# Compression blocks of two attention layers built by VectorE during the layer's projections, whose low weight parts VectorE also makes

## What is computed

```python
def nsa_mixer(h, w_in, cmp_pe, cmp_w1, cmp_w2, w_out):
    parts = jnp.split(h @ w_in, bounds, axis=-1)
    q = parts[0].reshape(B, T, NSA_KV, NSA_REP, NSA_DK)
    kc, vc, ks, vs, kw, vw = [p.reshape(B, T, NSA_KV, NSA_DK) for p in parts[1:7]]
    ...
    n_cmp = (T - CMP_LEN) // CMP_STRIDE + 1
    tok_idx = cmp_start[:, None] + jnp.arange(CMP_LEN)[None, :]

    def compress(a, j):
        blk = a[:, tok_idx] + cmp_pe[j][None, None, :, None, :]
        blk = jnp.moveaxis(blk, 3, 2).reshape(B, n_cmp, NSA_KV, CMP_LEN * NSA_DK)
        return jax.nn.gelu(blk @ cmp_w1[j]) @ cmp_w2[j]

    k_cmp = compress(kc, 0)
    v_cmp = compress(vc, 1)
```

## Time and profile before

| what | us or share |
|---|---|
| median of three runs | 3643.68 |
| lowest, highest | 3641.83, 3653.52 |
| the profiled execution's own time | 3645.8 |
| its span in the trace | 3644.0 |
| TensorE (PE) busy | 3038.3 (83%) |
| VectorE (DVE) busy | 2383.8 (65%) |
| ScalarE (ACT) busy | 1260.3 (35%) |
| GpSimd (POOL) busy | 590.9 (16%) |
| mean granted TensorE clock | 0.891 |

### The profile page before, as it was taken

The page is one execution under the profiler, slowest core; times in us unless marked ns, Lnnn a source line. Parts: engine busy times, 40 slices in busy tenths (PEclk is TensorE's granted clock), DMA queues, the critical chain, the costliest instruction groups (busy, mean ns, idle before and its releaser), DMA issues. The chain is left out here.

```text
span 3644.0 us, 52173 instructions
## 1 busy us (share of the span) xinstructions
PE 3038.3 (83%) x21162; PEld 2552.9 (70%) x21162; DVE 2383.8 (65%) x4291; ACT 1260.3 (35%) x2037; POOL 590.9 (16%) x321
## 2 busy tenths in 40 slices
PE   7977865565555699889999988999997999997899
PEld 4856752222211398868989876998986898987798
DVE  3677748888898687356767725877726775434654
ACT  1043211111111234264343445343345434343633
POOL 1010025555455100400000050000050000031000
PEclk9988777877767899879999987999997999996999
DMA  8932229999999786415758431867651764542153
GB/s 338 386 134 94 83 87 376 388 388 388 391 419 409 304 341 235 164 36 216 310 205 339 183 140 61 350 241 302 255 186 70 297 254 175 185 183 93 48 197 126
DMA packets 123103, 854.19 MB, mean 234 GB/s; under 512 B 17300, under 2 KB 18580, under 8 KB 21012
## 3 DMA queue, kind: packets, MB, share of 16 engines
q1 hardware_dynamic: 85748, 582.69, 41.7%
q0 software_dynamic: 36864, 268.45, 18.0%
q10 hardware_dynamic: 288, 0.26, 0.0%
HBM read 850.24 MB, written 1.11 MB: 234 GB/s over the span
## 5 line engine op out<-in xcount | busy, mean ns | idle before, releaser
L268 PE MATMUL ps<-h_hi,w_hi 128*128 128x256 f32 x3328 | 956.5, 287 | 51.8 <-DVE h_lo L459 26.2
L193 DVE TENSOR_TENSOR w_lo<-w_ring,w_hi 128x2048 fp32r<-128x2048 f32 x284 | 650.0, 2290 | 469.8 <-ACT w_hi L188 468.0
L269 PE MATMUL ps<-h_lo,w_hi 128*128 128x256 f32 x3328 | 952.0, 286 | 0.0
L270 PE MATMUL ps<-h_hi,w_lo 128*128 128x256 f32 x3328 | 951.7, 286 | 0.0
L188 ACT ACTIVATE w_hi<-w_ring 128x2048 fp32r<-128x2048 f32 x330 | 629.7, 1913 | 658.4 <-PE ps L270 646.5
L268 PEld LDWEIGHTS ps<-h_hi,w_hi 128*128 128x128 f32 x3328 | 645.1, 194 | 62.0 <-DVE h_lo L459 29.0
L269 PEld LDWEIGHTS ps<-h_lo,w_hi 128*128 128x128 f32 x3328 | 645.2, 194 | 3.2
L270 PEld LDWEIGHTS ps<-h_hi,w_lo 128*128 128x128 f32 x3328 | 644.8, 194 | 0.0
L193 POOL TENSOR_TENSOR w_lo<-w_ring,w_hi 128x2048 fp32r<-128x2048 f32 x46 | 212.2, 4631 | 2200.5 <-ACT w_hi L188 2200.5
L2937 PE MATMUL ps<-expert_rows,expert_diag 128*128 128x512 f32 x412 | 288.8, 841 | 231.2 <-ACT expert_diag L2978 231.2
L2937 PEld LDWEIGHTS ps<-expert_rows,expert_diag 128*128 128x128 f32 x412 | 92.2, 246 | 420.5 <-ACT expert_diag L2978 342.8
(11 more groups left out here) (461 smaller groups left out, 4232.2 us busy)
## 6 DMA issues: line engine op xcount, KB each, us to landing
w_ring<-in_w_stream SPq DMA_DIRECT2D x376, 1024.0 KB, 4.9
a_ring<-in_a_stream SPq DMA_DIRECT2D x108, 1024.0 KB, 7.0
a_ring<-in_t_stream SPq DMA_DIRECT2D x36, 1024.0 KB, 10.0
a_ring<-in_m_stream SPq DMA_DIRECT2D x8, 1024.0 KB, 7.3
alibi<-in_alibi SPq DMA_DIRECT2D x3, 2048.0 KB, 8.4
cond_row<-in_cond_row SPq DMA_DIRECT2D x8, 512.0 KB, 3.8
expert_rows<-in_experts,expert_idx POOLq DMA_INDIRECT x206, 11.8
gates<-mod_rows SPq DMA_DIRECT2D x3, 1024.0 KB, 5.1
```

The lines of the kernel that those rows point to most:

```text
L193: pool.tensor_tensor(self.w_halves(n)[1], self.w_item(n), self.w_halves(n)[0], ALU.subtract).then_inc(self.lo_made, 1)
L268: pe.matmul(out, stationary[0], moving[0], start=start, stop=False)
L269: pe.matmul(out, stationary[0], moving[1], start=False, stop=False)
L270: return pe.matmul(out, stationary[1], moving[0], start=False, stop=stop)
```

## The change

In the two `nsa` layers VectorE makes the low parts of items 3 to 10 during the projections, and GpSimd makes none there. VectorE puts each low part where ScalarE has the high one: ahead of unit n comes the low part of item n+3. The `cmp_blk` tile is taken before the projections. Behind its copy of unit 5 VectorE builds the 32 pieces of the keys' blocks (ScalarE's copy of unit 4 holds their source), and behind its copy of unit 7 the 32 pieces of the values' blocks. The compression block holds no additions and TensorE does not wait for blocks in it. The projections of the other two layers and the other stages are as before.

```diff
-def projections(core, items, units, side=None, split=True, ahead=S_AHEAD, tables=(), led=0, consts=()):
+def projections(core, items, units, side=None, split=True, ahead=S_AHEAD, tables=(), led=0, consts=(), beside=None):
...
         def copy(eng, parity):
-            ahead_of = splits if parity == 0 else range(0)
+            split = core.split_lo if parity else core.split_hi
+            ahead_of = splits if parity == 0 or beside else range(0)
             for u, (item, _, _, out) in enumerate(units):
                 while ahead_of and ahead_of[0] < first + item + S_SLOTS:
-                    core.split_hi(eng, ahead_of[0])
+                    split(eng, ahead_of[0])
                     ahead_of = ahead_of[1:]
...
                     out(eng, parity == 0, core.ps[:, u % BANKS, :]).then_inc(copied[parity].sem, 1)
+                    if beside and parity:
+                        beside(eng, u, copied)
             for n in ahead_of:
-                core.split_hi(eng, n)
+                split(eng, n)
...
-            for n in splits:
+            for n in () if beside else splits:
                 core.split_lo(pool, n)
...
+            blk = core.sb(early, "cmp_blk", [P, 2, CMP_LEN // 2, NSA_KV * N_CMP])
+
+            def blocks(dve, u, copied):
+
+                if u not in BLOCKS_BEHIND:
+                    return
+                i = BLOCKS_BEHIND.index(u)
+                for by in range(2):
+                    dve.wait_ge(copied[by].sem, copied[by].at(KEY_UNIT // 2 + 1))
+                if i == 0:
+                    dve.wait_ge(consts.sem, consts.at(32))
+                build_blocks(dve, blk, srcT, pe_col, i)
+
...
+KEY_UNIT = 4
+BLOCKS_BEHIND = (KEY_UNIT + 1, KEY_UNIT + 3)
+
+
+def build_blocks(dve, blk, srcT, pe_col, i):
+    for c in range(CMP_LEN // 2):
+        for up in range(2):
+            part = slice(up * DH, (up + 1) * DH)
+            t0 = 2 * c + up
+            src = srcT[i][part, :, t0:t0 + (N_CMP - 1) * CMP_STRIDE + 1:CMP_STRIDE]
+            dst = blk[part, i, c, :].rearrange("p (g n) -> p g n", g=NSA_KV)
+            dve.tensor_scalar(dst, src, pe_col[part, i, c:c + 1], None, ALU.add)
...
         @block.tensor
         def _(pe):
             for i in range(2):
-                pe.wait_ge(blocks.sem, blocks.at(i + 1))
                 for part in range(2):
```

More of the change, by code:

```diff
@@ L1545, in nsa_stage @@
             consts = core.semaphore_of("cmp_consts")
+            blk = core.sb(early, "cmp_blk", [P, 2, CMP_LEN // 2, NSA_KV * N_CMP])
[8 more added lines that the diff above has]
+                build_blocks(dve, blk, srcT, pe_col, i)
             projections(core, NSA_PROJ, units, ahead=0, tables=[(core.alibi[:], "alibi")], led=LEAD,
-                        consts=[(pe_col[:], core.io["cmp_pe"][j], consts), (w2[:], core.io["cmp_w2"][j], consts)])
-            compress(core, n, srcT, pe_col, w2)
+                        consts=[(pe_col[:], core.io["cmp_pe"][j], consts), (w2[:], core.io["cmp_w2"][j], consts)],
+                        beside=blocks)
+            compress(core, n, blk, w2)
             core.taken_whole()
@@ L1551, in nsa_stage, with compress @@
         out_projection(core, n.oT, 1, 1, 2, tail_room(core.alibi, n.ksT))
-def compress(core, n, srcT, pe_col, w2):
+KEY_UNIT = 4
[8 more added lines that the diff above has]
+            dve.tensor_scalar(dst, src, pe_col[part, i, c:c + 1], None, ALU.add)
+def compress(core, n, blk, w2):
     nc = core.nc
-    consts, blocks = core.semaphore_of("cmp_consts"), core.semaphore_of("cmp_blocks")
+    consts = core.semaphore_of("cmp_consts")
     hid, act_h, outs = core.semaphore_of("cmp_hid"), core.semaphore_of("cmp_act"), core.semaphore_of("cmp_outs")
@@ L1561, in compress @@
     nb = NSA_KV * N_CMP
-    chunks = CMP_LEN // 2
     with ExitStack() as ctx:
-        blk = core.sb(ctx, "cmp_blk", [P, 2, chunks, nb])
         hT = flat(n.oT)[:, 0:4 * nb].rearrange("p (i m n) -> p i m n", i=2, m=2)
@@ L1574, in _ @@
             core.dve_steps.done(dve, dve.memset(n.vcmp[:], 0.0))
[L1575 to L1584, removed]
             for i in range(2):
@@ L1637, in compress @@
     consts.passed(32)
-    for s in (blocks, hid, act_h, outs):
+    for s in (hid, act_h, outs):
         s.passed(2)
```

## The result

| | before | the change |
|---|---|---|
| median (lowest to highest), us | 3643.53 (3641.37 to 3653.52), 8 executions | 3628.81 (3610.00 to 3633.64), 8 executions |
| ratio to before, 95% interval | | 0.9949 (0.9937 to 0.9961) |
| profiled execution: time, span, us | 3645.8, 3644.0 | 3625.27, 3623.5 |

The kernel is 0.5% faster, 14.7 us. The forecast was 28 us, for a clock that holds through the compression in both layers. Half of that came: it is the time of the rival "holds in one layer" (3627), and the trace shows that rival, layer by layer.

What follows compares the result with a forecast made beforehand. TensorE's standing still, chiefly 10.45 us a layer for `cmp_blk`, and its half-clock compression were taken as the bound; +7.3 - 9.3 + 1.7 - 13.8 = -14.1 us a layer gave 3615.5 us, range 3608 to 3640.

Steps and rivals of the forecast that it cites:

- holds in one layer: Compression: full clock kept in one layer, lost at the other's entry; -17 us in all, 3627 us; chance 0.20.
- the one with 0.55: Compression: the clock holds at 1.00 through both halves in both layers, giving 3615.5 us; chance 0.55.
- VectorE's chain: Projections: low parts of items 8 and 10 queue behind additions, TensorE stalls 3.5 and 4.9 us; +7.3 us a layer.
- The clock in the projections: Item 10, behind the second stall: a stretch at half clock loses 1.7 us a layer, bounds 0 and 3.4.
- The entry: Between projections and compression: the wait of 10.45 us becomes a gap of 1.15; -9.3 us a layer.
- The compression's speed: Compression at full clock: 7.0 us a half, at most 8.1; 27.8 us become 14.0, -13.8 us a layer.
- The rule that I set against it: Compression: two operand loads a record take 213 ns at either clock, so no gain there and a sum nearly zero.
- Whether the clock holds: Compression: granted clock taken to stay at 1.00, from the expert stage's 34 us of bursts; the -13.8 us a layer needs it.
- what the rival said of a fall: Compression: clock falls after 2 to 5 us, gaining about 2.5 us a layer; in both layers 3638 us; chance 0.17.
- Additions run longer beside the projections: VectorE's two runs of 32 in the projections: at about 370 ns an addition, not 280, 3655 us; chance 0.05.
- one of my signs of a wrong mechanism: VectorE in the projections: 32 additions lasting longer than 9 us would show the mechanism wrong.
- the forecast's own range: Whole kernel: 3609 (no clock loss in item 10, faster tail) to 3622 us (126 ns a record, long low stretch).

Runs made afterwards that it cites:

- The first experiment: The change with the low parts made by GpSimd again and the additions still in the projections; median 3647.14 us, ratio 1.0006 to the kernel before.

## Why the prediction was right and where it failed

The sign and the range were right: 3628.81 lies in 3608 to 3640. The forecast itself, 3615.5, was missed by 13 us, and the case with 0.20 came in place of the one with 0.55.

*VectorE's chain* held to a tenth of a microsecond. The stage began 3.05 us earlier in this execution; less that, I had the low part of item 8 at 1508.55 (TensorE went on at 1508.51), that of item 10 at 1524.95 (1524.95) and the end of item 10 at 1532.45 (1532.43). The second stall is 3.33 us and not 4.9 because the clock fell behind the first and item 8 ended later, which the prediction had said would cost nothing.

*The clock in the projections.* +1.7 us was right for the first layer (18 matmuls in 3.3 us behind the second stall). In the last it was the lower bound, 0: the six microseconds before the compression are all at 1.00. Projections and entry together: -0.65 and -2.1 us where I had -0.3.

*The entry* is 0.80 us, taken as 1.15.

*The compression's speed* at full clock: 14.8 us for 128 records, 116 ns a record, between my 109 and the bound of 126. The rule that I set against it, from the Trainium skill's "TensorE: Matmul & The Clock Gate" (LDWEIGHTS), has a load time without the clock in it and gives no gain; here the trace decides against it:
```profile
L1633 PEld LDWEIGHTS ps<-cmp_blk,w_ring x256: 186/192/333, 1533.2 to 3311.7; 128*128 128x128 f32 x128
L1633 PE MATMUL ps<-cmp_blk,w_ring x256: 275/275/437, 1533.2 to 3311.8; 128*128 128x60 f32 x128
```
These are durations in ns, lowest, median and highest. Loads of 192 ns are those at full clock, of 333 those at half. The two lines also show one load for each record, 256 and 256, where I had counted two.

*Whether the clock holds*: this is the step that failed, "this row is nearer than the other, and I take that it holds, in both halves and both layers". With its tail the compression became 14.4 us shorter in the last layer, as forecast (-13.8), and 2.25 us in the first, which is what the rival said of a fall (-2.5). I had written both rows down, one of a fall 3 us behind a dense stretch and one of 34 us of bursts at 1.00, and let the nearer one speak for both layers. The right reading was the one that I gave to the rival: the pause at the entry and the sparse loop lie together in the same few microseconds, so the start is where the fall is to be looked for, once per layer. Of three profiles with an entry of 0.80 us and nothing dense behind it, the first layer lost the clock in all and the last in none. I had called the difference between the layers "chance in the true sense"; three profiles with the same order speak against that. That the median fell so near this rival's 3627 was to this extent luck: its mechanism was right, but nothing in my working said that one layer of the two would fall, or which.

*The rivals.* "Additions run longer beside the projections" was rightly rare for this change, but the danger is real: with GpSimd busy they take 698 ns each. The change avoids it only by moving the low parts as well. Taken to the letter, one of my signs of a wrong mechanism was there, as 32 additions took 9.09 us where I had set 9 as the mark; GpSimd had no work beside them, and 0.1 us is no sign of the danger. In the working, the upper end of the forecast's own range, 3622, should be 3623: 4.4 us for 126 ns a record and 3.4 for the long low stretch.

**What stays open.** Why the first layer falls and the last does not: the two have the same order of work and the same gap. Nor is it shown whether the one execution of 3610.0 us had both compressions fast, which its time suggests, as it has no profile. Its mean granted clock, 0.898 where the other seven show 0.891 to 0.895, says that it spent less time at 0.50, but not where. The first experiment's executions run from 3636.6 to 3651.1 us; why their median lies 6.5 us above what its stages say is open too.

## What to carry to other kernels

Before small additions are put beside other work, ask which engine's work they exclude: VectorE's adds on SBUF operands stood still under GpSimd's, and ScalarE's did not. In a list that runs in order, put what TensorE needs next ahead of the long run, then share that run by the measured price per piece until every engine ends before TensorE does. And where a sparse loop starts behind a pause, look at the clock in its first microseconds; eight matmuls whose result nobody uses, at 1.8 us, made the first layer's stage 10.3 us shorter (82.66 to 72.34) and the last one's, which had not lost the clock, 1.7 us longer (70.60 to 72.34).

## What the runs showed that I had not expected

- VectorE's 64x60 additions beside GpSimd's subtractions: 22.34 us for 32 in place of 8.95, while GpSimd's kept 4.6 us each.
- ScalarE needs 408 ns for the same addition, 124 more than VectorE, so that 64 of them took longer than the slack that ScalarE seemed to have.
- In none of the 28 profiled compressions did the granted clock change after the first 3 us. At 0.50 it stayed down for 34 us, with dense matmuls in the loop, though TensorE was busy for 33.95 of 34.1; at 1.00 it stayed up for all of 14.6.
